# One decoder kernel: token scales of cross attention applied to the logits, all MLP blocks in joined products, norm scales behind the split parts

## What is computed

```python
def rmsnorm_2(x, g):
    y = xf * lax.rsqrt(jnp.mean(xf * xf, axis=-1, keepdims=True) + EPS)
    return (y * g.astype(jnp.float32)).astype(x.dtype)

def mem_cross_attn(h, m, w_q, w_kv, w_o):
    q = (h @ w_q).reshape(B, S, MEM_HEADS, MEM_HEAD_DIM)
    s = jnp.einsum('bqhd,bmhd->bhqm', q, kv[:, :, 0]) * MEM_HEAD_DIM ** -0.5
    p = jax.nn.softmax(s, axis=-1)

def sq_relu_mlp(h, w_in, w_out):
    return jnp.square(jax.nn.relu(h @ w_in)) @ w_out
```

## Time and profile before

| what | value |
|---|---|
| median of 3 runs | 957.87 us (957.31 to 958.57) |
| span of the profiled execution | 955.0 us |
| TensorE busy | 943.5 us, 99% of the span |
| VectorE busy | 641.3 us, 67% |
| ScalarE busy | 542.0 us, 57% |
| GpSimd busy | 48.5 us, 5% |
| HBM read | 157.11 MB, 166 GB/s over the span |

### The profile page before, as it was taken

How to read it: one execution, slowest core, us unless ns; L and a number is a source line. 1 busy time by engine, 2 the same in 40 slices (tenths; PEclk the granted TensorE clock), 3 DMA queues, 4 the chain that set the end, 5 groups by cost and what they waited for, 6 DMA issues and landing times.

```text
span 955.0 us, 14502 instructions
## 1 busy us (share of the span) xinstructions
PE 943.5 (99%) x5508; PEld 821.8 (86%) x5508; DVE 641.3 (67%) x1256; ACT 542.0 (57%) x1033; POOL 48.5 (5%) x99
## 2 busy tenths in 40 slices
PE   9999999999999999999999999999999999999997
PEld 7878888888788998989888888899988898888886
DVE  5888674877677686668666556477864767555654
ACT  6686673757676655566444444465663666444442
POOL 3001340002010000000000000000000000000000
PEclk9999999999999999999999999999999999999999
DMA  9886525554534464445566557664355255655551
GB/s 285 256 198 125 168 91 172 176 177 133 163 93 122 114 182 151 150 134 176 177 185 203 185 179 246 179 188 136 133 175 176 89 177 185 204 185 179 199 174 44
DMA packets 112320, 159.10 MB, mean 167 GB/s; under 512 B 13854, under 2 KB 49020, under 8 KB 112124
## 3 DMA queue, kind: packets, MB, share of 16 engines
q1 hardware_dynamic: 111816, 157.62, 53.2%
q10 hardware_dynamic: 436, 0.56, 0.2%
HBM read 157.11 MB, written 1.06 MB: 166 GB/s over the span
## 4 chain that ended last, share of the span: by engine, by line
PE 93%; DVE 2%; ACT 2%; DMA 1%; issue 1%; SPq 1%; DVEq 0%; ACTq 0%
PE bank L490 23%; PE bank L492 22%; PE bank L491 22%; PE bank L1185 9%; PE bank L1186 5%; PE bank L632 3%; PE bank L646 2%; PE bank L544 2%; PE bank L658 2%; DMA raw<-in_w_in_ab 1%; PE bank L617 1%; PE bank L1324 1%; SPq L2696 1%; DVE w_lo L1927 0%; DVE xT L1985 0%
## 5 line engine op out<-in xcount | busy, mean ns | idle before, releaser
L1927 DVE TENSOR_TENSOR w_lo<-raw,w_hi 128x1024 fp32r<-128x1024 f32 (+1 forms) x294 | 335.6, 1185 | 136.5 <-ACT w_hi L1402 136.1
L1402 ACT CAST w_hi<-raw 128x1024 fp32r<-128x1024 f32 (+1 forms) x294 | 283.3, 1021 | 133.3 <-DMA raw<-in_mlp_w_in 72.9
L490 PE MATMUL bank<-w_hi,xT 128*128 128x512 f32 (+1 forms) x366 | 145.3, 397 | 1.2 <-issue 0.8
L492 PE MATMUL bank<-w_hi,xT 128*128 128x512 f32 (+1 forms) x366 | 141.3, 386 | 0.0
L491 PE MATMUL bank<-w_lo,xT 128*128 128x512 f32 (+1 forms) x366 | 140.8, 385 | 0.0
L490 PE MATMUL bank<-w_hi,hT_hi 128*128 128x512 f32 (+1 forms) x348 | 136.9, 393 | 0.3
L1185 PE MATMUL bank<-xT,w_hi 128*128 128x512 f32 x384 | 136.0, 398 | 0.0
L492 PE MATMUL bank<-w_hi,hT_lo 128*128 128x512 f32 (+1 forms) x348 | 134.9, 388 | 0.0
L491 PE MATMUL bank<-w_lo,hT_hi 128*128 128x512 f32 (+1 forms) x348 | 134.7, 387 | 0.0
L1186 PE MATMUL bank<-xT,w_lo 128*128 128x256 f32 x384 | 107.8, 281 | 0.0
L490 PE MATMUL bank<-xT,w_hi 128*128 128x256 f32 x368 | 106.0, 288 | 0.4 <-DVE w_lo L1927 0.3
(11 more groups left out here) (270 smaller groups left out, 1343.7 us busy)
## 6 DMA issues: line engine op xcount, KB each, us to landing
raw<-in_mlp_w_in SPq DMA_DIRECT2D x32, 1024.0 KB, 5.3
raw<-in_mlp_w_out SPq DMA_DIRECT2D x32, 1024.0 KB, 5.1
raw<-in_w_in_ab SPq DMA_DIRECT2D x13, 1024.0 KB, 11.0
raw<-in_w_in_cd SPq DMA_DIRECT2D x13, 1024.0 KB, 5.1
raw<-in_xa_w_kv SPq DMA_DIRECT2D x8, 1024.0 KB, 5.1
raw<-in_sb_w_qkv SPq DMA_DIRECT2D x16, 512.0 KB, 4.7
raw<-in_w_out_ab SPq DMA_DIRECT2D x4, 1024.0 KB, 5.0
raw<-in_w_out_cd SPq DMA_DIRECT2D x4, 1024.0 KB, 5.1
```

Source lines behind the costliest of these rows:

```text
L490: pe.matmul(o, wh, ih, start=start, stop=False, skip_group_check=True)
L492: return pe.matmul(o, wl, ih, start=False, stop=stop, skip_group_check=True)
L1402: nc.scalar.copy(w_hi[:, u % SLOTS, a], raw[:, u % SLOTS, a]).then_inc(hi_ready, 1)
L1927: V.tensor_tensor(w_lo[:, u % SLOTS, a], raw[:, u % SLOTS, a], w_hi[:, u % SLOTS, a].bitcast(F32), ALU.subtract).then_inc(lo_ready, 1)
```

## The change

Five edits are made together:

1. Cross attention's queries are multiplied by a constant, and the token's scale is applied to the logits, as the per-token factor of the instruction that makes them (L2136 before). `row_scales`, `row_copy` and the waits for them go. The mask operand, which was a zero block of `causal`, is now a row block of `alibi` that GpSimd clears.
2. MLP blocks 0 and 1 use `up`, with banks 4 to 7 for each block, and their units arrive in the order block 0, block 1. Block 1 waits for `relu_ready` of block 0, as all blocks now do for the block before. The turn of the norm's second half stands after half of block 0's first unit.
3. For the norms of cross attention and MLP (`LATE_SCALES`) the split parts of the second half come before the sums of squares and the scales, on ScalarE and VectorE.
4. `values_T` makes one matmul of 256 columns and one of 128 in place of three of 128.
5. The fox heads' row of scales is made for 8 partitions in place of 128.

The diff, with most unchanged lines and ScalarE's part of edit 5 left out:

```diff
@@ -167,9 +168,8 @@
                 add(("down", i, b, n), UNIT, (0, 4, PANEL, PANEL, wout[:, 4 * b:4 * b + 4, n * PANEL:(n + 1) * PANEL]))
-        for n in range(2):
-            up(0, (n,))
-            up(1, (n,))
+        up(0)
+        up(1)
         down(0)
@@ -396,7 +396,7 @@
             if k["kind"] == "xa":
-                k["tab"] = lambda a, b: causal[:, P:2 * P].unsqueeze(1).to_broadcast([P, 2, P])
+                k["tab"] = lambda a, b: alibi[:, 0, 0:S]
@@ -572,12 +572,12 @@
-            def row_scales(name, b):
+            def row_scales(name, b, m=P):
                 for t in range(T):
-                    ins = pe.matmul(banks[b][:, t * P:(t + 1) * P], rs(name, t).to_broadcast([P, P]), ident[:, :], start=True, stop=True)
+                    ins = pe.matmul(banks[b][0:m, t * P:(t + 1) * P], rs(name, t).to_broadcast([P, m]), ident[:, :], start=True, stop=True)
                 end(("R", name), ins, (row_ready, row_no[name]))
@@ -668,9 +668,8 @@
                 else:
-                    pe.matmul(o[:, 0:P], v(0), pt[:, 0:P], start=True, stop=True)
-                    pe.matmul(o[:, P:S], v(0), pt[:, P:S], start=True, stop=False)
-                    ins = pe.matmul(o[:, P:S], v(1), pt[:, S:S + P], start=False, stop=True)
+                    pe.matmul(o, v(0), pt[:, 0:S], start=True, stop=False, skip_group_check=True)
+                    ins = pe.matmul(o[:, P:S], v(1), pt[:, S:S + P], start=False, stop=True, skip_group_check=True)
                 state["loT"] += 1
@@ -1090,7 +1089,6 @@
                 part(("xq", i, 1), us[1], (1, 2), True, False, r)
-                row_scales(("c", i), 3)
                 ks = heads_of("xa", layer=i)
@@ -1158,29 +1156,23 @@
-                def up_half(odd, n, u):
-
-                    A_ = 4 + 2 * odd
-                    take(u)
-                    for f in range(4):
-                        o = banks[A_ + f // 2][:, (f % 2) * S:(f % 2 + 1) * S]
-                        for c in range(4):
-                            a = [flat(w, u)[:, c * BLK + f * P:c * BLK + (f + 1) * P] for w in (w_hi, w_lo)]
-                            ins = three(o, a, [v[:, 4 * n + c, :] for v in X], u, n == 0 and f % 2 == 0 and c == 0, n == 1 and c == 3)
-                        if n == 1 and f == 1:
-                            ins.then_inc(written[A_], 1)
-                    ins.then_inc(units_used, 1)
-
                 def up(u, blk):
                             b = 4 + f
-                            if n == 0:
-                                pe.wait_ge(relu_ready, relu0 + 4 * (blk - 2) + f + 1)
+                            if n == 0 and blk:
+                                pe.wait_ge(relu_ready, relu0 + 4 * (blk - 1) + f + 1)
+                            if n == 0 and blk == 0:
+                                begin(("upbank", b), b)
+                                base[b] = uses[b]
+                            if n == 0 and blk == 0 and f == 2:
+                                turn_x(("p", i), 1, 0)
                             for c in range(4):
                                 k = 4 * n + c
+                                if blk == 0 and f == 0:
+                                    pe.wait_ge(*r(k))
                                 wh, wl = (flat(w, u + n)[:, c * BLK + f * P:c * BLK + (f + 1) * P] for w in (w_hi, w_lo))
-                for odd in range(2):
-                    for b in (4 + 2 * odd, 5 + 2 * odd):
-                        begin(("upbank", b), b)
-                        base[b] = uses[b]
-                    pe.wait_ge(*r(3))
-                    up_half(odd, 0, u0 + odd)
-                    if odd == 0:
-                        turn_x(("p", i), 1, 0)
-                pe.wait_ge(*r(KC - 1))
-                for odd in range(2):
-                    up_half(odd, 1, u0 + 2 + odd)
+                for blk in range(2):
+                    up(u0 + 2 * blk, blk)
                 down(0, u0 + 4, 0, True, False)
                     down(1 - blk % 2, u + 2, blk - 1, False, False)
-                for b, n in ((4, NBLK - 1), (5, NBLK - 2), (6, NBLK - 1)):
-                    uses[b] += n
+                for b in (4, 5, 6):
+                    uses[b] += NBLK
                 for b in (4, 5, 6, 7):
@@ -1482,11 +1465,15 @@
                 for half in range(2):
+                    late = half and name[0] in LATE_SCALES
+                    if late:
+                        hi_T((name, half), 4, xT_hi, 4 * half)
                     for t in range(T):
                         rsqrt(stat[name], T)
-                    hi_T((name, half), 4, xT_hi, 4 * half)
+                    if not late:
+                        hi_T((name, half), 4, xT_hi, 4 * half)
                     if half == 0 and before is not None:
@@ -1793,7 +1780,6 @@
                 used(before)
-                row_copy(("c", i))
                 used(U[("xq", i, 0), 0])
@@ -1821,16 +1807,9 @@
                     splits(u + 6 if blk else u + 5)
-                    for p in range(2 if blk < 2 else 0):
-                        b = 4 + 2 * odd + p
-                        if p == 0:
-                            act.wait_ge(written[b], mlp_base[i][b] + 1)
-                        else:
-                            act.wait_ge(units_used, max(u + 2, u0 + 3))
-                        nc.scalar.activation(pan(4, p), banks[b][:, :], ACT.Relu).then_inc(relu_ready, 1)
-                    for f in range(4 if blk >= 2 else 0):
+                    for f in range(4):
                         if f < 3:
-                            act.wait_ge(written[4 + f], mlp_base[i][4 + f] + blk - f % 2)
+                            act.wait_ge(written[4 + f], mlp_base[i][4 + f] + blk + 1)
                         else:
@@ -2031,8 +2010,13 @@
                 residual(last, 1)
-                norm_scales(name)
-                lo_chunks((name, 1), 4, X, 4)
+                if name[0] in LATE_SCALES:
+                    lo_chunks((name, 1), 4, X, 4)
+                    own.settle()
+                    norm_scales(name)
+                else:
+                    norm_scales(name)
+                    lo_chunks((name, 1), 4, X, 4)
                 own.settle()
@@ -2124,6 +2108,8 @@
                     dve.wait_ge(table_ready, k["table"] + 1)
+                if k["kind"] == "xa":
+                    dve.wait_ge(table_ready, len(tables) + 1)
                 if g >= 2:
                     tab, o, i_ = k["tab"](a, z), k["nl"][:, a:z], ps[:, a:z]
-                    if k["kind"] == "xa":
-                        o, i_ = (v.rearrange("p (a b) -> p a b", a=2) for v in (o, i_))
-                    ins = V.tensor_tensor_reduce(o, i_, tab, -k["scale"], BIG * 1e8, ALU.add, ALU.min, nmax[:, 2 * g + t:2 * g + t + 1])
+                    scale = neg_rs(("c", k["layer"]), t) if k["kind"] == "xa" else -k["scale"]
+                    ins = V.tensor_tensor_reduce(o, i_, tab, scale, BIG * 1e8, ALU.add, ALU.min, nmax[:, 2 * g + t:2 * g + t + 1])
                     if k["kind"] == "swa":
@@ -2455,18 +2440,17 @@
                 x_turned(("c", i), last, before)
-                dve.wait_ge(row_ready, row_no["c", i])
                     ps = condition(dve, ("xq", i, 0))
-                    own.sig(V.tensor_tensor(two_halves(pan(0, 0)), two_halves(ps[:, :]), row2, ALU.mult), xq_ready)
+                    own.sig(V.tensor_scalar(pan(0, 0), ps[:, :], P ** -0.5, None, ALU.mult), xq_ready)
                     a = slice(n * S, (n + 1) * S)
-                    own.sig(V.tensor_tensor(pan(0, 1)[:, a], ps[:, a], row[:, :], ALU.mult), xq_ready)
+                    own.sig(V.tensor_scalar(pan(0, 1)[:, a], ps[:, a], P ** -0.5, None, ALU.mult), xq_ready)
@@ -2501,15 +2485,11 @@
                             dve.wait_ge(hT_ready, h0 + 2 * blk)
-                        if blk < 2:
-                            dve.wait_ge(relu_ready, relu0 + 2 * blk + p + 1)
-                            V.tensor_tensor(pan(5, p), pan(4, p), pan(4, p), ALU.mult).then_inc(h_ready, 1)
-                            continue
                         for f in (2 * p, 2 * p + 1):
                             o = pan(4, p)[:, f % 2 * S:(f % 2 + 1) * S]
-                            dve.wait_ge(second_ready, second0 + 4 * (blk - 2) + f + 1)
+                            dve.wait_ge(second_ready, second0 + 4 * blk + f + 1)
                             V.tensor_tensor(o, banks[4 + f][:, 0:S], o, ALU.add).then_inc(relu_ready, 1)
-                            own.last = (relu_ready, relu0 + 4 * (blk - 1) + f + 1)
+                            own.last = (relu_ready, relu0 + 4 * blk + f + 1)
                         own.settle()
```

More of the change, by code:

```diff
@@ L46 @@
 NBLK = DFF // BLK
-RELUS = 4 + 4 * (NBLK - 2)
+RELUS = 4 * NBLK
 MLA_QL, MLA_KVL, NOPE, ROPE, MLA_V = 384, 256, 128, 64, 128
@@ L50 @@
 TWO_PI_HI = 6.28125
+LATE_SCALES = ("c", "p")
 MLA_PANELS = (4, 5, 7, 8, 9)
@@ L433, in build @@
         norm_no = {name: n + 1 for n, name in enumerate(order_of_norms)}
```

(12 more changed lines are left out.)

2 lines of the change are left out of this document (1 added, 1 removed).

## The result

The changed kernel takes **968.31 us** (median of 4 runs, 967.47 to 968.85) beside 957.59 us for the kernel before (median of 4): ratio 1.0116, 95% interval 1.0104 to 1.0128, so slower, by 10.7 us. Forecast were 965.6 us, with a range up to 968.2. The profiled execution spans 966.9 us.

A forecast was written before the change was run, and what follows sets the result against it. TensorE, busy 943.5 of 955.0 us, was taken to bound the kernel. Gap +7.6, transposes +0.2, cross attention +1.1, joined products -0.9 and values -0.3 make +7.7: span 962.7, time 965.6 us, range 962.7 to 968.2.

The forecast's parts named there:

- The gap: Between MLP blocks 0 and 1, TensorE waits for VectorE's first addition behind six w_lo: 3.8 us per MLP, +7.6.
- The clock in the gap: Rival: granted clock falls in the MLP gap; one fall gives 968.1 us, two 970.6; chance 0.13.
- a fall in both gaps: Sign that the prediction is wrong: the clock falls in both MLPs' gaps; two falls would give 970.6 us.
- The range: Whole kernel's time, 962.7 to 968.2 us: the forecast's own range with one fall of the clock.
- My own upper bound without a fall: Whole kernel's time with gaps up to 4.2 us and cross attention within its bounds: 966.9 us at most.
- my 968.1 for one fall: Whole kernel's time if the clock falls in one MLP gap: 968.1 us, against 965.6 without a fall.
- The price of a fall: After an MLP gap, about 5 us at half pace, 2.5 us lost per fall, taken from the program's start.
- The level: Whole kernel: the 2.9 us between profiled span (955.0 us) and median (957.87 us) are kept as they are.
- Joined products: MLP blocks 0 and 1: a joined pair takes 0.353 us against 0.36, over 128 groups 0.9 us less.
- Transposes' wait: In each MLP's block 0, four transposes wait 0.1 us for the residual: +0.2 for both MLPs.
- Cross attention: TensorE waits 0.7 us for queries behind the late scales' chain; each cross attention 0.55 us longer, +1.1 for two.
- Value products: Latent or stick-breaking heads: values take 0.65 us instead of 0.67, over 16 heads 0.3 us less.

The follow-up runs named there:

- run 1: Changed kernel with block 0's additions, and ScalarE's copies, placed ahead of four of the six low parts: 957.11 us, ratio 0.9996.
- run 7: Changed kernel with block 0's additions behind four low parts instead of six, x_turned's wait for the last unit kept: 960.11 us, ratio 1.0036.
- run 2: Changed kernel with 14 float32 products that nothing reads run while TensorE waits between blocks 0 and 1 of each MLP: 965.0 us, ratio 1.0079.
- run 11: Changed kernel with block 0's additions ahead of four of six low parts and scales early in both cross attention and MLP: 955.42 us, ratio 0.998.
- run 3: Changed kernel with the MLP's scales ahead of the second half's split parts again, cross attention keeping the new order: 965.82 us, ratio 1.0086.
- run 4: Changed kernel with cross attention's scales ahead of the second half's split parts again, the MLP keeping the new order: 966.19 us, ratio 1.0089.
- run 6: Kernel before with only the joined 512-column products in MLP blocks 0 and 1, scales still ahead of the low parts: 963.91 us, ratio 1.007.

## Why the prediction was right and wrong

- **The gap (forecast 3.8 us, twice).** Right in place, cause and size. TensorE was ready at 437.2 and restarted at 441.06; the walk through the changed queues gave 437.2 and 441.0. Runs 1 and 7 show the cause: with four or two of the `w_lo` moved behind the addition, the gap is gone or 2.3 us shorter.
- **The clock in the gap (a rival, chance 0.13). This is the step that failed.** I took from the earlier trace rows that 3.4 us without a product leave the clock at full and 3.8 are the edge. But those rows are one fall, of an engine that did not come back. They tell when the level changed that time, not how long the idle stretch had to be, and the time itself varies: at the program's end the clock fell 2.1 us behind the last product in run 2 and some 5.2 behind it in run 11, and no trace lies outside these two:

```profile
956.50:958.50 2.00, 0.00 (x0) 0.00 (x0) 1.07 (x5) 1.61 (x8) 1.03 (x1) 1.00 0.20 72
958.60:961.00 2.40, 0.00 (x0) 0.00 (x0) 1.28 (x4) 0.72 (x1) 0.00 (x0) 0.50 0.02 6
```

```profile
948.20:953.30 5.10, 0.00 (x0) 0.00 (x0) 2.39 (x9) 2.44 (x9) 1.06 (x1) 1.00 0.20 76
953.50:954.90 1.40, 0.00 (x0) 0.00 (x0) 0.00 (x0) 0.00 (x0) 0.00 (x0) 0.50 0.42 154
```

Behind the gaps of 2.5 us and more it fell in eight of eight, in both MLPs of the changed kernel and of runs 3, 4 and 6, in five of them only after TensorE was back. It held behind 1.56 us (run 7) and 0.70 (run 2), both times in both MLPs. So a fall in both gaps, which I had named as a sign of being wrong, was what came. The Trainium skill's "TensorE: Matmul & The Clock Gate", Part 1, has the throttled state as the default that activity releases; these traces agree, with VectorE busy throughout the gap and TensorE's clock falling.
- **The range.** Its upper end, 968.2, is the likeliest time plus one fall. My own upper bound without a fall, 966.9, and one fall make 969.4, so the range was narrower than I described it. And 968.3 lies beside my 968.1 for one fall by luck: there were two falls, and other terms took back what the second cost.
- **The price of a fall (2.5 us).** Ten steps of a pair at 0.64 instead of 0.35 us are 2.9 us in the first MLP, six are 1.6 in the second. The six falls of runs 3, 4 and 6 cost 1.4 to 1.6 each, so that is the usual price here, and the 2.5 from the program's start was too high. With 4.5 us for both, the sum would have given a span of 967.2; it was 966.9.
- **The level.** I kept 2.9 us between span and median. In each run of the changed kernel 1.75 to 1.85 us lie around the span, so before's profiled execution was about 1 us below its median; the unsteady waits early in the program are of that size. This is why the clock's 4.5 us came out as a miss of only 2.7: 1.1 us were added too many here, 0.4 is the changed kernel's median below its profiled execution, and 0.3 is the first 300 us, which came out 0.55 shorter, with the terms below.
- **Joined products (-0.9).** Under-sized. In block 0 the pairs came at 0.346 (22 in 7.62 us, 429.09 to 436.71), in block 1 at 0.353 once the clock was full. The groups of three they replace took 0.361 (48 in 17.35 us, 431.60 to 448.95). That is 0.7 us per MLP, 1.5 in all; the best runs, at 0.347 throughout, have 0.9 per MLP.
- **Transposes' wait (+0.2).** 0.96 us for eight where it was 0.79: +0.17 in each MLP, 0.3 in all.
- **Cross attention (+1.1).** The wait was 0.62 us (forecast 0.7) and VectorE began the queries at 401.32 against the 402.0 worked out minus the 0.71 us by which the whole execution was ahead. The stage was 0.70 and 0.68 longer, 0.3 in all more than the sum had. Run 4 shows the cause: with the chain back in its place both become 0.3 shorter, so the late chain costs 1.0 each.
- **Value products (-0.3).** Right: 0.65 us a head, 0.25 us in all.

Open: why the half clock lasted some 6.8 us in the first MLP of the changed kernel and 3.4 in each of the seven other falls, with the same products behind it. The idle time doesn't decide it (3.83 us in run 4 as well). The fall came earliest there, 0.7 us before TensorE was back; in run 4 it came 0.2 and 0.4 before, in the other five 0.1 to 0.9 after. Whether that is the cause, no run shows. It may not be the only such execution: the mean granted clock was 0.993 in the two longer of the changed kernel's four (968.67 and 968.85 us) and 0.994 in the two shorter.

## What to carry to other kernels

A bank that is freed by another engine's work needs that work early in the other engine's queue; where bulk work stands in front of it, move the one instruction that TensorE waits for, and what feeds it on the third engine. A new gap costs more than its length once the clock follows it down: here a gap of 1.6 us made the MLPs 2.0 and 1.4 us longer than in run 1, and gaps of 2.5 us or more cost 1.4 to 1.6 us on top, once 2.9. And an order that hides a chain behind a wait (late scales) is good or bad by where that wait lies: in the MLP it cost 1.8 us in the old order, 1.3 us of gap in the joined one, and nothing once the addition was moved. That the joined products (7.1 us) and the rest (4.9) come to 12.0 us alone and 10.7 together is within the intervals of the times; by the traces the MLPs lose 11.6 and 11.5 us. The same parts became a gain of 2.2 us once two places in the queues were mended.

## What the runs showed of the hardware

The granted clock fell after a pause of 2.5 us that ended before the fall: TensorE worked 0.9 us at full clock behind it, and then some six pairs ran at or near half (run 3). Products that nothing reads, run in the gap, kept it at full (run 2).

The same joined pair, 768 columns, has two paces at full clock, 0.347 and 0.354 us, and keeps one of them through a whole block with no wait and no change of the granted clock. The code alone doesn't decide which one it is: the two MLPs of run 1, which have the same code, ran 54 pairs at 0.347 and 54 at 0.353. Over an MLP's first two blocks that is 0.45 us. I had taken 0.353 as the price of a pair from the earlier trace rows, and the later joined blocks keep to it in every trace. What sets the pace stays open.
